# Index rows as the first column chunk with selection rounds moved forward, and stick-breaking remainders from split parts of L

## What is computed

```python
a = rmsnorm(h, g_attn)
qa, ka, va, qi, ki, wi, qb, kb, vb, u = split_columns(a @ w_in)
qa = rope(rmsnorm(qa, g_q_a), pos); ka = rope(rmsnorm(ka, g_k_a), pos)
qi = rope(qi, pos); ki = rope(ki, pos)
# group A: the top k keys by an index score, then softmax attention over them
score[t, s] = sum_h wi[t, h] * relu(qi[t, h] . ki[s] / 8)       # 4 index heads
_, sel = top_k(where(causal, score, -inf), 128)                 # prompt: 128 keys
o_a = softmax over sel of (qa . ka / 8), times va               # 6 heads on 2 KV heads
# group B: stick-breaking attention, strictly causal, 6 heads
z = qb . kb / 8
rev = reverse cumulative sum over keys of log_sigmoid(-z)
o_b = exp(z + rev) @ vb
# group C: pooling over trailing windows, a small linear map
h += concat(o_a, o_b, o_c) @ w_out
h += ConvFFN(rmsnorm(h)); h += sigmoid(rmsnorm(h) @ w_ple_gate) * (p @ w_ple_proj)
```

## Time and profile before

| | |
|---|---|
| median of 3 runs | 1616.64 us (1613.22 to 1617.04) |
| the profiled execution | 1620.47 us, its span 1618.7 us |
| TensorE busy | 1556.1 us (96%), mean granted clock 0.984 |
| VectorE busy | 883.4 us (55%) |
| ScalarE busy | 683.5 us (42%) |
| GpSimd busy | 276.4 us (17%) |
| chain that ended last | TensorE 79%, VectorE 13%, ScalarE 3%, issue 3% |

### The profile page before, as it was taken

The page is one execution under the profiler, slowest core; times in us unless marked ns, Lnnn a source line. Parts: engine busy times, 40 slices in busy tenths (PEclk is TensorE's granted clock), DMA queues, the critical chain, the costliest instruction groups (busy, mean ns, idle before and its releaser), DMA issues.

```text
span 1618.7 us, 30649 instructions
## 1 busy us (share of the span) xinstructions
PE 1556.1 (96%) x11772; PEld 1415.8 (87%) x11772; DVE 883.4 (55%) x1534; ACT 683.5 (42%) x995; POOL 276.4 (17%) x474
## 2 busy tenths in 40 slices
...
GB/s 166 66 99 87 34 142 110 53 66 91 91 90 89 80 87 100 92 81 85 79 69 77 138 40 58 105 98 86 72 91 91 91 78 91 98 88 92 84 70 61
DMA packets 225719, 140.24 MB, mean 87 GB/s; under 512 B 13122, under 2 KB 219604, under 8 KB 225552
## 3 DMA queue, kind: packets, MB, share of 16 engines
...
## 4 chain that ended last, share of the span: by engine, by line
PE 79%; DVE 13%; ACT 3%; issue 3%; POOL 1%; DMA 0%; DVEq 0%; SPq 0%; ACTq 0%; POOLq 0%
PE ps L1714 23%; PE ps L1716 22%; PE ps L1715 22%; DVE score L1379 3%; DVE m L1376 3%; DVE w_L L1270 2%; PE ps L2065 1%; PE ps L1994 1%; DVE Lb L1451 1%; PE ps L1741 1%; PE ps L1797 1%; PE ps L1905 1%; PE ps L1767 1%; PE ps L2149 1%; PE ps L1907 1%
## 5 line engine op out<-in xcount | busy, mean ns | idle before, releaser
L1714 PE MATMUL ps<-bH,w_H 128*128 128x272 f32 x1664 | 481.1, 289 | 4.7 <-DVE w_L L1270 3.2
L1270 DVE TENSOR_TENSOR w_L<-w_raw,w_H 128x1024 fp32r<-128x1024 f32 (+4 forms) x236 | 257.6, 1100 | 414.1 <-ACT w_H L890 411.3
L1716 PE MATMUL ps<-bH,w_L 128*128 128x272 f32 x1664 | 479.6, 288 | 0.0
L1715 PE MATMUL ps<-bL,w_H 128*128 128x272 f32 x1664 | 477.9, 287 | 0.0
L890 ACT ACTIVATE w_H<-w_raw 128x1024 fp32r<-128x1024 f32 (+4 forms) x236 | 220.1, 943 | 270.1 <-PE ps L1716 269.4
L1714 PEld LDWEIGHTS ps<-bH,w_H 128*128 128x128 f32 x1664 | 312.6, 188 | 6.3 <-DVE w_L L1270 4.1
L1715 PEld LDWEIGHTS ps<-bL,w_H 128*128 128x128 f32 x1664 | 313.6, 188 | 0.1
L1716 PEld LDWEIGHTS ps<-bH,w_L 128*128 128x128 f32 x1664 | 312.6, 188 | 0.0
L1714 PE MATMUL ps<-actH,w_H 128*128 128x272 f32 x704 | 204.2, 290 | 0.0
L1716 PE MATMUL ps<-actH,w_L 128*128 128x272 f32 x704 | 203.8, 289 | 0.0
L1715 PE MATMUL ps<-actL,w_H 128*128 128x272 f32 x704 | 202.7, 288 | 0.0
...
## 6 DMA issues: line engine op xcount, KB each, us to landing
...
```

The lines of the kernel that those rows point to most:

```text
L1270: ins = dve.tensor_tensor(w_L[u % SPLIT][:, a:b], w_raw[raw_slot(l, u)][:, a:b], w_H[u % SPLIT][:, a:b].bitcast(F32), ALU.subtract)
L1714: pe.matmul(out, wh, xh, start=start, stop=False)
L1715: pe.matmul(out, wh, xl, start=False, stop=False)
L1716: return pe.matmul(out, wl, xh, start=False, stop=stop)
```

## The change

The index columns (with the v of group A) become chunk 0, the q and k of group A chunk 1. Their index products move into chunk 1, the index scores and the first 13 selection rounds on VectorE ahead of the first logits; of the other 35 rounds, 8 stand in the softmax loop. The rotations run in the order index(0..4), qk(0..4), with qk(4) behind the split of unit 13. Gains are multiplied into two tables for cosine and sine (`rot_q`, `rot_k`) instead of into the rows, and ScalarE squares the rows. Both decode steps of a chunk follow k = 5. In the stick-breaking part, L is split: ScalarE copies the high part, VectorE subtracts for the low part, and the remainders are summed in single passes (fp32r) from both. One half of a feature moves ahead of the remainders in turns 0 and 1. SyncE's part is not changed.

```diff
-CHUNK = [(0, 512), (512, 964), (1732, 2116)]
+CHUNK = [(512, 964), (0, 512), (1732, 2116)]
-CH_BLOCKS = [(F_QA, 4), (F_QI, 3)]
+CH_BLOCKS = [(F_QI, 3), (F_QA, 4)]
-        I_BANK = [7, 0]
+        I_BANK = [3, 4]
...
-pool.tensor_scalar(gains[:, 0, :], gains[:, 0, :], 0.125, None, ALU.mult)
-pool.wait_ge(hs_rec, at(hs_rec, 1))
+pool.tensor_scalar(gains[:, 0, :], gains[:, 0, :], 0.125, None, ALU.mult).then_inc(pool_step, steps.step())
+pool.wait_ge(pool_step, steps.value())
 hold(pool)
+for g, out in ((0, rot_q), (1, rot_k)):
+    gn = gains[:, g, :].unsqueeze(1)
+    cs, sn = (dcon[:, d:d + TILES * HD].rearrange("p (t d) -> p t d", d=HD) for d in (D_COS, D_SIN))
+    pool.tensor_tensor(out[:, 0, :, :], cs, gn.to_broadcast([P, TILES, HD]), ALU.mult)
+    for a in (0, 32):
+        pool.tensor_tensor(out[:, 1, :, a:a + 32], sn[:, :, a:a + 32],
+                           gn[:, :, 32 - a:64 - a].to_broadcast([P, TILES, 32]), ALU.mult)
 for t in range(TILES):
-    n = TOKW[t]
     pool.wait_ge(p_ev, at(p_ev, t + 1))
-    x = x_tok[0:n, t, :].rearrange("p (h d) -> p h d", d=HD)
-    pool.tensor_tensor(x, x, hstat[0:n, t, :].unsqueeze(2).to_broadcast([n, 8, HD]), ALU.mult).then_inc(pool_step, steps.step())
-    pool.wait_ge(pool_step, steps.value())
     hold(pool)
-    pool.tensor_tensor(x[:, 0:6, :], x[:, 0:6, :], gains[0:n, 0, :].unsqueeze(1).to_broadcast([n, 6, HD]), ALU.mult)
-    pool.tensor_tensor(x[:, 6:8, :], x[:, 6:8, :], gains[0:n, 1, :].unsqueeze(1).to_broadcast([n, 2, HD]), ALU.mult).then_inc(qk_ok, 1)
-for t in range(TILES):
+    store("a_v", t, "n d", V[:, t, 0:128], kv_out)
     pool.wait_ge(rope_ok, at(rope_ok, t + 1))
     hold(pool)
-    store("a_k", t, "n d", r_tok[:, t, 384:512], ak_out)
-for t in range(TILES):
-    pool.wait_ge(p_ev, at(p_ev, 5 + t + 1))
-    hold(pool)
-    store("a_v", t, "n d", V[:, t, 0:128], kv_out)
-    pool.wait_ge(rope_ok, at(rope_ok, 5 + t + 1))
-    hold(pool)
     store("idx_k", t, "d", r_tok[:, t, 256:320], ix_out)
-for t in range(TILES):
-    pool.wait_ge(p_ev, at(p_ev, 10 + t + 1))
-    hold(pool)
-    store("b_v", t, "n d", V[:, t, 128:512], kv_out)
 for t in range(1, 4):
     pool.wait_ge(i_sc, at(i_sc, 4 * t))
     hold(pool)
     blk = score_of(t)[:, P * t:P * t + P]
     pool.affine_select(out=blk, in_=blk, compare_op=ALU.is_ge, fill=MASKED, base=0,
                        pattern=[[-1, P]], channel_multiplier=1).then_inc(i_diag, 1)
+pool.wait_ge(hs_rec, at(hs_rec, 1))
+hold(pool)
+for t in range(TILES):
+    n = TOKW[t]
+    pool.wait_ge(p_ev, at(p_ev, 5 + t + 1))
+    x = x_tok[0:n, t, :].rearrange("p (h d) -> p h d", d=HD)
+    pool.tensor_tensor(x, x, hstat[0:n, t, :].unsqueeze(2).to_broadcast([n, 8, HD]), ALU.mult).then_inc(qk_ok, 1)
+for t in range(TILES):
+    pool.wait_ge(rope_ok, at(rope_ok, 5 + t + 1))
+    hold(pool)
+    store("a_k", t, "n d", r_tok[:, t, 384:512], ak_out)
+    pool.wait_ge(p_ev, at(p_ev, 10 + t + 1))
+    hold(pool)
+    store("b_v", t, "n d", V[:, t, 128:512], kv_out)
...
     if c == 0:
         if t == 0:
             act.wait_ge(n_rec, at(n_rec, 1))
-        ins = copy(x_tok[0:n, t, :], src, r)
+        copy(V[0:n, t, 0:128], src[:, 0:128], r)
+        ins = copy(x_tok[0:n, t, 0:324], src[:, 128:452], r)
     elif c == 1:
-        copy(V[0:n, t, 0:128], src[:, 0:128], r)
-        act.wait_ge(rope_ok, at(rope_ok, t + 1))
-        ins = copy(x_tok[0:n, t, 0:324], src[:, 128:452], r)
+        act.wait_ge(rope_ok, at(rope_ok, 5 if t == 0 else t + 1))
+        if t >= 2:
+            act.wait_ge(hs_ss, at(hs_ss, t - 1))
+        copy(x_tok[0:n, t, :], src, r)
+        ins = act.activation((t1, t2)[t % 2][0:n, :], src, ACT.Square, scale=r)
...
 part_copy(0)
-for t in range(TILES):
+leave(0, 0)
+split(5)
+for t in range(1, TILES):
     leave(0, t)
-split(5)
-act.wait_ge(hs_ss, at(hs_ss, 1))
-inverse(hstat[:, :, :], hstat[:, :, :]).then_inc(hs_rec, 1)
 act.wait_ge(u_tr, at(u_tr, 1))
 for m in range(2):
     ins = copy(u_s[:, m, :, 0:15], ps[:, 7, 128 * m:128 * m + 120].rearrange("p (b r) -> p b r", r=15))
 ins.then_inc(ph_ev, 1)
 split(6)
+turned(0, 0)
+turned(0, 1)
+turned(0, 2)
 split(7)
-turned(0, 0)
+turned(0, 3)
+turned(0, 4)
+relu(1, 0, 4)
 split(8)
 part_copy(1)
-turned(0, 1)
-for t in range(3):
-    leave(1, t)
+relu(2, 0, 4)
+relu(3, 0, 4)
+leave(1, 0)
+leave(1, 1)
 split(9)
-turned(0, 2)
+leave(1, 2)
 leave(1, 3)
-turned(0, 3)
 leave(1, 4)
 split(10)
-turned(0, 4)
-turned(1, 0)
+act.wait_ge(hs_ss, at(hs_ss, 5))
+inverse(hstat[:, :, :], hstat[:, :, :], 1.0 / HD).then_inc(hs_rec, 1)
 split(11)
-turned(1, 1)
-turned(1, 2)
+part_copy(2)
 split(12)
-part_copy(2)
-turned(1, 3)
-turned(1, 4)
-for t in range(2):
-    leave(2, t)
+leave(2, 0)
+leave(2, 1)
 split(13)
 for t in range(2, TILES):
     leave(2, t)
-for t in range(1, 4):
-    relu(t, 0, 4)
-    split(U_F + t + 1)
+turned(1, 0)
+turned(1, 1)
+split(14)
+turned(1, 2)
+turned(1, 3)
+split(15)
+turned(1, 4)
+split(16)
...
+def stick_high(h):
+    act.wait_ge(b_dve, at(b_dve, 4 * (h // 2) + h % 2 + 1))
     if h >= 2:
         act.wait_ge(b_o, at(b_o, h - 1))
+    copy(L_high[:, h % 2, :], Lb[:, h % 2, :]).then_inc(b_act, 1)
...
     stick_ln(e1, r1)
-    split(U_F + 2 * q + 5)
     if q == 0:
         act.wait_ge(ak_out, at(ak_out, 5 * 16))
         act.wait_ge(ix_out, at(ix_out, 5 * 16))
+    stick_high(e0)
+    stick_high(e1)
+    split(U_F + 2 * q + 5)
...
 def head_squares(t):
 
     n = TOKW[t]
-    dve.wait_ge(p_ev, at(p_ev, t + 1))
-    dve.scalar_tensor_tensor(t1[0:n, :], x_tok[0:n, t, :], 1.0 / HD, x_tok[0:n, t, :], ALU.mult, ALU.mult).then_inc(dve_step, steps.step())
-    dve.wait_ge(dve_step, steps.value())
-    total = dve.tensor_reduce(hstat[0:n, t, :], t1[0:n, :].rearrange("p (h d) -> p h d", d=HD), AX.X, ALU.add)
-    if t < TILES - 1:
-        total.then_inc(dve_step, steps.step())
-        dve.wait_ge(dve_step, steps.value())
-    else:
-        total.then_inc(hs_ss, 1)
+    dve.wait_ge(p_ev, at(p_ev, 5 + t + 1))
+    dve.tensor_reduce(hstat[0:n, t, :], (t1, t2)[t % 2][0:n, :].rearrange("p (h d) -> p h d", d=HD), AX.X, ALU.add).then_inc(hs_ss, 1)
...
+        groups = [(0, 6, rot_q[0:n, 0, t, :], rot_q[0:n, 1, t, :]), (6, 8, rot_k[0:n, 0, t, :], rot_k[0:n, 1, t, :])]
+    else:
+        groups = [(0, heads, *(dcon[0:n, d + 64 * t:d + 64 * t + 64] for d in (D_COS, D_SIN)))]
     a = t1[0:n, 0:w].rearrange("p (h d) -> p h d", d=HD)
     b = t2[0:n, 0:w].rearrange("p (h d) -> p h d", d=HD)
-    dve.tensor_tensor(a, x, cs, ALU.mult)
-    dve.tensor_tensor(b[:, :, 0:32], x[:, :, 32:64], sn[:, :, 0:32].to_broadcast([n, heads, 32]), ALU.mult)
-    dve.tensor_tensor(b[:, :, 32:64], x[:, :, 0:32], sn[:, :, 32:64].to_broadcast([n, heads, 32]), ALU.mult).then_inc(dve_step, steps.step())
+    for h0, h1, cs, sn in groups:
+        m = h1 - h0
+        cs, sn = cs.unsqueeze(1), sn.unsqueeze(1)
+        dve.tensor_tensor(a[:, h0:h1, :], x[:, h0:h1, :], cs.to_broadcast([n, m, HD]), ALU.mult)
+        dve.tensor_tensor(b[:, h0:h1, 0:32], x[:, h0:h1, 32:64], sn[:, :, 0:32].to_broadcast([n, m, 32]), ALU.mult)
+        ins = dve.tensor_tensor(b[:, h0:h1, 32:64], x[:, h0:h1, 0:32], sn[:, :, 32:64].to_broadcast([n, m, 32]), ALU.mult)
+    ins.then_inc(dve_step, steps.step())
...
     dve.wait_ge(qk_ok, at(qk_ok, t + 1))
+    dve.wait_ge(t_mm, at(t_mm, t + 1))
+    dve.wait_ge(ix_out, at(ix_out, 5 * 16))
+    hold(dve)
...
 dve.wait_ge(hs_one, at(hs_one, 1))
+index(0)
+split(5)
+index(1)
+index(2)
+split(6)
+index(3)
+index(4)
+split(7)
+weigh(1, 0, 2)
+weigh(1, 2, 4)
+select(1, 0, 2)
+split(8)
+weigh(2, 0, 2)
+weigh(2, 2, 4)
+select(1, 2, 3)
+weigh(3, 0, 2)
+weigh(3, 2, 4)
+select(1, 3, 4)
 head_squares(0)
+split(9)
 head_squares(1)
 head_squares(2)
-split(5)
 head_squares(3)
 head_squares(4)
-split(6)
+split(10)
+select(1, 4, 7)
+split(11)
 qk(0)
-split(7)
 qk(1)
-split(8)
+split(12)
 qk(2)
 qk(3)
-split(9)
+split(13)
 qk(4)
-index(0)
-split(10)
-index(1)
-split(11)
-index(2)
-index(3)
-split(12)
-index(4)
-split(13)
-weigh(1, 0, 2)
 feature_out(0)
-weigh(1, 2, 4)
 split(14)
-select(1, 0, 2)
-weigh(2, 0, 2)
-select(1, 2, 3)
-weigh(2, 2, 4)
+select(1, 7, 9)
 feature_out(1)
 split(15)
-select(1, 3, 5)
-weigh(3, 0, 2)
-select(1, 5, 6)
-weigh(3, 2, 4)
+select(1, 9, 13)
 feature_out(2)
 split(16)
...
+for i, m in enumerate((ntri, nones)):
+    ins = dve.tensor_copy(con_r[:, P * i:P * i + P], m)
...
+def stick_low(h):
+    dve.wait_ge(b_act, at(b_act, 4 * (h // 2) + h % 2 + 3))
+    lo(L_low[:, h % 2, :], Lb[:, h % 2, :], L_high[:, h % 2, :]).then_inc(b_dve, 1)
...
-select(1, 6, 11)
+select(1, 13, 16)
+select(2, 0, 2)
 stick_max(0)
+feature_out(3)
 stick_max(1)
-feature_out(3)
+stick_low(0)
+stick_low(1)
 split(17)
-select(1, 11, 16)
-select(2, 0, 7)
+select(2, 2, 7)
 feature_out(4)
 split(18)
-select(2, 7, 10)
+select(2, 7, 11)
 stick_max(2)
+feature_out(5)
 stick_max(3)
-feature_out(5)
+stick_low(2)
+stick_low(3)
 split(19)
-select(2, 10, 16)
-select(3, 0, 4)
+select(2, 11, 16)
 feature_out(6)
```

(66 more changed lines are left out.)

48 lines of the change are left out of this document (29 added, 19 removed).

## The result

The changed kernel takes 1657.78 us in the median of four runs (1656.51 to 1660.17), the kernel before beside it on the same chip 1616.84: a ratio of 1.025, 95% interval 1.0233 to 1.0267. It is slower by 41 us. I had forecast 1641.6, at most 1653. The direction and the gate came out; the rest of the loss, some 6.4 us a layer for which I had put 1.3, did not.

The account below looks back on a forecast made before the run. VectorE was taken to bound the attention part from unit 16's split to selection's end. Selection ending 11 us later plus 1.5 of clock gave 12.5 a layer, 25 in all: 1641.6 us, range 1619 to 1653.

Parts of the forecast that it names:

- the gate: Before the logits: late qk(4) and SyncE's pages delay unit 16, its split ending at 142.1 instead of 132.3; chance 0.72.
- the stretch: VectorE's fixed list from the split of unit 16 to the end of selection: 92.3 us before, 93.6 forecast.
- The cover: Stick-breaking turns 0 and 1: half a feature, 3.1 us, moved ahead covers the 2.7 us longer chain before the first remainder.
- about 1 more of idle: VectorE, split of unit 16 to end of selection: about 1 us of idle time added in the 93.6 us sum.
- wasn't the bound: Sign that the forecast is wrong: VectorE idle in many small pieces after 150 us.
- Rounds in the softmax: Softmax loop: eight rounds instead of 3, adding 5 x 1.74 = 8.7 us there, which the part before it has less of.
- Rival D: Softmax rounds starve TensorE and its clock stays low to the decode part: 5 us more a layer, 1655; chance 0.04.
- Single passes: Remainders: 2.7 us a head instead of 4.35, saving 9.8 us a layer of TensorE time alone.
- TensorE's savings there are worth only what VectorE lets through: From the split of unit 16 to the end of selection: VectorE's 92.3 us list, with about 3 us idle, limits any gain.
- Ahead of the logits: Chunks and features before the first logits: chunk 2 ends at about 106, logits at 128.5 instead of 131.3, 2.8 us earlier.

Follow-up runs that it names:

- e1: Changed kernel with SyncE asking for units 16 to 19 before the wait for the tenth rotation and the 16 index pages: 1629.56 us.
- e2: Changed kernel with feature_out(3) directly behind split(16) on VectorE and feature_out(5) ahead of stick_max(2): 1655.45 us.
- e11: e1 with the half feature back behind the remainders in turns 0 and 1, as in the kernel before: 1644.85 us.
- e5: e1 with VectorE's list reordered, no work added: rounds moved into holes and ahead of the logits, six instead of eight in the softmax: 1619.53 us.
- e3: Changed kernel with five of the eight softmax-loop rounds of tile 3 moved back in front of the loop: 1654.01 us.
- e10: Kernel before with only the high and low part of L and the single-pass remainders added: 1635.75 us, ratio 1.0103.
- e7: e1 with the f32 remainders of the kernel before, no high and low part of L: 1636.24 us.
- e12: e9 with the f32 remainders of the kernel before, no high and low part of L: 1619.09 us.
- e6: e5 with relu(2, 0) and relu(2, 1) before the split of unit 8, and chunk 2's first decode step behind k = 3: 1614.74 us.
- e9: e6 with all four relu of tile 2 and their weighing before the split of unit 8, unit 12 split between the first two rotations: 1610.32 us.

## Why the prediction was right about the gate and short on the time

*The gate: right.* The chain was qk(4), SyncE's pages, unit 16, split, rounds, clip. Unit 16 was to be asked for at 136.5 (138.6 measured), its split to end at 142.1 (144.7). The agreement is partly luck: the first rotation started at 103.0, not 99, and the rotations (1.2 us) and SyncE (0.7) were faster than forecast. Split(11) began only at 100.51, behind three rounds, and took 2.55 beside GpSimd's multiplications, which I had costed beside qk(0) alone:

```profile
100.51 2.55 DVE L1300 TENSOR_TENSOR w_L<-w_raw,w_H 128x384 fp32r<-128x384 f32 x2
102.99 1.40 DVE L1354 TENSOR_TENSOR t<-x_tok,rot_q 128x384 f32<-128x384 f32 x1
104.31 1.19 DVE L1355 TENSOR_TENSOR t<-x_tok,rot_q 128x192 f32<-128x192 f32 x1
105.42 0.34 DVE L1356 TENSOR_TENSOR t<-x_tok,rot_q 128x192 f32<-128x192 f32 x1
```

qk(0) took 4.1 us (102.99 to 107.07), not 4.7, and the later ones 2.3: two of its six products are slowed, by 0.84 us each (0.56 and 0.35 in qk(1)), and the others start after GpSimd is done, at 105.3. The Trainium skill ("SBUF — State Buffer", section "Terms") lets the loser of the shared port block for the whole instruction, by which I had put qk(0) at up to 3 us more; the trace has less of it, since only two products met GpSimd. Of my 12.5 us a layer, 11.3 were for this gate (9.8 of delay, 1.5 of clock) and the rest for the stretch behind it; e1 measures 14 for the gate.

*The cover: wrong in the explanation, without a price.* I wrote that half a feature "covers that in turns 0 and 1". Nothing in my working asked what frees its bank. It stands behind the wait of 12.76, not in it; e2 shows that this is worth 1 us a layer under the gate, e11 that the same half is worth 7.6 without it. TensorE's wait was 12.76 us, not some 9, and the first remainders came at 158.9, not 154.3: about half of that is the low part, ready at 156.7, the other half the half feature (154.03 to 158.92, with a mean granted clock of 0.60), which stood ahead of them.

*The step that failed: "-8.5 + 8.4 + 0.4 + about 1 more of idle = 93.6 us instead of 92.3".* The stretch took 102.8 us (144.7 to 247.5), and the term that failed most is "about 1 more of idle". Together with the 2.6 of the gate that is the whole distance of the end of selection from the forecast, 247.5 for 235.7. The columns of both windows are us, PE, PEld, DVE, ACT, POOL, then PEclk, DMA share and GB/s; first the kernel before, then the changed one:

```profile
132.30:224.70 92.40, 85.75 (x556) 64.69 (x552) 78.12 (x172) 45.56 (x65) 27.01 (x39) 0.98 0.21 62
```
```profile
144.70:247.50 102.80, 80.62 (x503) 62.08 (x504) 82.77 (x163) 53.67 (x77) 33.42 (x57) 0.82 0.26 73
```

VectorE's busy time grew by 4.7 us and its other time by 5.7. The sum had +2.3 and -1 for them: a round is busy for 0.93 of its 1.21 us, so seven rounds take off 6.5 and 2.0, and low parts, constants and "about 1 more of idle" come on top. Of the 9.2 us that the sum lacks, some 2.4 are busy time (a split and a low part beside GpSimd alone took 2.06 and 2.31 us for 1.22 and 1.41), and 6.7 are idle time. The premise was that VectorE stays the bound through the stretch. It does not: with the rounds taken out, it comes to the end of its work in turns 0 and 1 ahead of TensorE and waits for it.

```profile
170.19 0.72 DVE L1422 SCALAR_TENSOR_TENSOR featT<-ps,r_all 128x544 f32<-128x544 f32 x1 [3.81 <-PE ps L1762]
...
196.87 0.44 DVE L1428 TENSOR_TENSOR u_p<-ps,r_all 128x272 f32<-128x272 f32 x1 [3.01 <-PE ps L1762]
```

The gate and the low clock behind it add to this, but do not make it. In e1 the gate is gone and turn 0 has the full clock. VectorE's rows there, then its stretch:

```profile
156.91 0.72 DVE L1424 SCALAR_TENSOR_TENSOR featT<-ps,r_all 128x544 f32<-128x544 f32 x1 [1.99 <-PE ps L1764]
...
183.60 0.44 DVE L1430 TENSOR_TENSOR u_p<-ps,r_all 128x272 f32<-128x272 f32 x1 [3.01 <-PE ps L1764]
```
```profile
133.30:233.80 100.50, 84.21 (x572) 66.50 (x570) 82.65 (x163) 54.88 (x78) 33.42 (x57) 0.92 0.26 75
```

It still takes 100.5 us, so 6.9 of the 9.2 us stand without the gate. My sign for a VectorE that "wasn't the bound" was idle time "in many small pieces after 150"; it came as two large ones.

A fixed list is as long as its sum only without holes. Against the stretch ahead of the softmax it shows best: 132.3 to 212.6 before is 80.3 us; 144.7 to 225.7 after is 81.0, although 8.5 + 8.7 us of rounds had left it and 8.8 of low parts and constants had come. So 9 us were lost in it, and the softmax part, 7.0 us longer for the rounds it took over, was not paid back. e5 brought back 5 us a layer with the same work in another order. How much of that is holes filled and how much is rounds moved out of the softmax was not measured apart.

*Rounds in the softmax: nearly right.* 1.74 each, in layer 0 an even exchange (e3). Rival D, a softmax that starves TensorE and holds its clock low, had at most a small part, 2 us a layer by e3. The clock in the softmax is 0.84 after and 0.93 in e1, and the part takes 52.4 us in both.

*Single passes: sized right, judged right for the wrong kernel.* A pair of heads took 5.50 us (158.92 to 164.42), 2.75 a head against 2.7 forecast and 4.35 before. Four products of 512 to 128 columns take 0.64 us, the six narrower ones, with the same 1280 columns, 0.75:

```profile
161.64 0.80 PE L1957 MATMUL ps<-L_high,con_r 128*128 128x512 f32 x4
162.28 0.80 PE L1957 MATMUL ps<-L_low,con_r 128*128 128x512 f32 x4
162.92 0.92 PE L1961 MATMUL ps<-L_high,con_r 128*128 128x384 f32 x6
163.67 0.91 PE L1961 MATMUL ps<-L_low,con_r 128*128 128x384 f32 x6
164.42 0.34 PE L1760 MATMUL ps<-aH,w_H 128*128 128x272 f32 x1
```

The Trainium skill ("TensorE: Matmul & The Clock Gate", section "Back-to-back issue gap") gives 81 ns for 128 columns, from which I had estimated 2.5 for a head; the trace has 2.75. "TensorE's savings there are worth only what VectorE lets through" is true of the kernel before (e10, 9 us a layer lost) and false once the rounds have moved out and the rest of the change is in place (e7 3.4, e12 4.4 us a layer gained): there VectorE is the one with idle time. I judged the part by the old balance though the change altered it.

*Ahead of the logits: too bright.* The wait for a relu (2.53; 2.4 forecast) and the one for unit 12 (1.54; 1) were seen, the 1.90 us at 34.31 in chunk 0 were not; chunk 2 ended at 108.4, not 106, and the logits came at 132.2, not 128.5. For unit 12 I had the wrong reason in part: VectorE's place for the split (e6, e9) ended it as well as the load.

*What is open.* e1 gave 14 us a layer by the medians, 13.3 in turn 0 of layer 0, and 17.8 by the distance from layer to layer. The 17.8 are of one execution each: 1.6 us less from layer 0's pages to layer 1's logits, 13.2 in turn 0, 1.2 in turn 2, 1.8 in the softmax. Why the last two and the stretch ahead differ was not traced. The early rounds and the moved index products were never run by themselves, so no run gives their price. Whether a better order of VectorE's list than e9's exists was not tried.
